# Causal term of the diagonal blocks on VectorE, and closing products right behind the input products

## The reference

```python
def causal_attention(q, k, v):          # 12 heads, q and k 96 wide (64 + 32 rotated), v 64 wide
    ...
    sc = jnp.einsum('bqhd,bkhd->bhqk', q_blk, k) * scale
    mask = k_pos[None, :] <= q_pos[:, None]
    p = jax.nn.softmax(jnp.where(mask[None, None], sc, -jnp.inf), axis=-1)
    return jnp.einsum('bhqk,bkhd->bqhd', p, v)

def rg_lru_branch(u, ...):              # 768 channels, 6 tiles of 128
    ...                                 # xc: causal convolution with 4 taps
    r = jax.nn.sigmoid(xb @ w_r + b_r)
    i = jax.nn.sigmoid(xb @ w_i + b_i)
    log_a = (-8.0 * softplus(-lam)) * r
    gated_x = jnp.sqrt(-jnp.expm1(2.0 * log_a)) * (i * xc)
    # h_t = exp(log_a)_t * h_{t-1} + gated_x_t
```

## Time and profile before

| | |
|---|---|
| median of 3 runs | 3370.74 us (3360.85 to 3375.93) |
| the profiled execution: its own time, its span | 3378.57 us, 3376.4 us |
| busy share of the span: PE, DVE, ACT, POOL | 91%, 39%, 29%, 24% |
| mean granted clock of PE | 0.941 of full speed |
| token attention, first rotation to last product | 2419 to 2820 us |
| inputs and closing products of the recurrent layer | 2999 to 3169 us |

### The profile page before, as it was taken

One profiled execution on the slowest core, in us unless ns is written; L12 is line 12 of the kernel. 1 busy time (PEld: TensorE's weight loads), 2 busy tenths in 40 slices (PEclk: granted clock), 3 DMA queues, 4 the chain that ended last, 5 costly groups with the idle time before them and its releaser, 6 DMA issues. The chain is left out here.

```text
span 3376.4 us, 33623 instructions
## 1 busy us (share of the span) xinstructions
PE 3083.4 (91%) x14024; PEld 2306.9 (68%) x14024; DVE 1305.8 (39%) x1342; ACT 974.6 (29%) x1262; POOL 808.8 (24%) x380
## 2 busy tenths in 40 slices
PE   8899999999989798899999999898699999888896
PEld 3677777877766476688888787676466666666555
DVE  5153111333426443300000245321656663539455
ACT  3232222212133123311111344231234341336212
POOL 1223111215332122312121345331021111223100
PEclk9999999999989898899999999998799999899898
DMA  9311111252132342111111233312100001120201
GB/s 353 135 51 63 50 50 56 106 174 76 63 138 80 109 167 71 48 50 47 46 45 48 75 125 112 103 56 78 56 20 13 19 20 69 56 75 32 91 13 50
DMA packets 76486, 261.01 MB, mean 77 GB/s; under 512 B 8049, under 2 KB 12385, under 8 KB 75329
## 3 DMA queue, kind: packets, MB, share of 16 engines
q1 hardware_dynamic: 76352, 259.13, 21.8%
HBM read 207.10 MB, written 51.99 MB: 77 GB/s over the span
## 5 line engine op out<-in xcount | busy, mean ns | idle before, releaser
L277 POOL TENSOR_TENSOR w_lo_sb<-raw_w_sb,w_hi_sb 128x1024 fp32r<-128x1024 f32 x231 | 577.9, 2503 | 2061.6 <-ACT w_hi_sb L268 2061.5
L268 ACT ACTIVATE w_hi_sb<-raw_w_sb 128x1024 fp32r<-128x1024 f32 x231 | 243.1, 1052 | 437.7 <-PE ps L285 401.6
L285 PE MATMUL ps<-merged_parts_hi_sb,w_hi_sb 128*128 128x512 f32 x832 | 335.3, 403 | 23.0 <-PEq L500 12.5
L285 PE MATMUL ps<-merged_parts_lo_sb,w_hi_sb 128*128 128x512 f32 x832 | 330.6, 397 | 0.0
L285 PE MATMUL ps<-h_hi_sb,w_hi_sb 128*128 128x512 f32 x720 | 295.7, 411 | 17.7 <-PEq L872 10.7
L285 PE MATMUL ps<-h_lo_sb,w_hi_sb 128*128 128x512 f32 x720 | 288.8, 401 | 0.0
L285 PE MATMUL ps<-merged_parts_hi_sb,w_lo_sb 128*128 128x512 f32 x832 | 275.3, 400 | 0.0
L285 PE MATMUL ps<-h_hi_sb,w_lo_sb 128*128 128x512 f32 x720 | 245.4, 401 | 0.0
L285 PE MATMUL ps<-z_lo,w_hi_sb 128*128 128x512 f32 x512 | 207.3, 405 | 0.0
L285 PEld LDWEIGHTS ps<-merged_parts_hi_sb,w_hi_sb 128*128 128x128 f32 x832 | 158.2, 190 | 67.3 <-issue 19.0
L2732 DVE TENSOR_TENSOR ffn_hidden_sb<-ffn_hidden_sb,ps 128x1024 f32 x20 | 24.4, 1221 | 431.6 <-PE ps L285 431.6
(11 more groups left out here) (571 smaller groups left out, 5579.2 us busy)
## 6 DMA issues: line engine op xcount, KB each, us to landing
raw_w_sb<-in_w SPq DMA_DIRECT2D x231, 512.0 KB, 3.2
ada_w_sb<-in_ada SPq DMA_DIRECT2D x48, 512.0 KB, 6.7
inbox_sb<-gates_out SPq DMA_DIRECT2D x24, 512.0 KB, 4.1
gates_out<-outbox_sb SPq DMA_DIRECT2D x16, 512.0 KB, 2.6
inbox_sb<-sums_out SPq DMA_DIRECT2D x16, 512.0 KB, 4.7
spilled_sum<-x_sb SPq DMA_DIRECT2D x32, 256.0 KB, 2.0
x_sb<-spilled_sum SPq DMA_DIRECT2D x2, 4096.0 KB, 13.7
x_sb<-in_x SPq DMA_DIRECT2D x4, 1024.0 KB, 11.7
```

The lines of the kernel that those rows point to most:

```text
L268: nc.scalar.activation(w_hi[:, n % RING].rearrange("p t m -> p (t m)"), raw_w[:, n % RAW], ACT.Copy).then_inc(w_rounded.sem, 1)
L277: nc.gpsimd.tensor_tensor(w_lo[:, n % RING].rearrange("p t m -> p (t m)"), raw_w[:, n % RAW], flat_hi, ALU.subtract).then_inc(w_split.sem, 1)
L285: mm = nc.tensor.matmul(o, wt, xs, start=start and part == 0 and xs is x_hi, stop=stop and part == 1)
```

## The change

In the attention:
- The mask product of a diagonal step is gone. DVE adds the constant in PSUM instead (`causal_term`), and ACT's Exp of such a step waits for DVE (`causal_s`).
- The steps of the second half take blocks 4 to 7 first, so that the first eight steps of a head are the diagonal ones.
- `weigh` runs two steps behind the scores instead of one, and `maxima` comes ahead of `weigh`.
- The rotation of the queries (`turn_queries`) writes the rounded tile by a sum of its own instead of a cast. For heads 0 and 1 it stays in its place; for the others it moves from P(u+1) into S(u), behind the causal terms of the first two steps.
- DVE's order in S(u): eight causal terms with the rotation behind the second and six maxima behind the last six, `normalise(u, 0)`, the last two maxima.

In the recurrent layer: `closing` is planned from the end of `inputs`, and the roundings and subtractions of `gating` are planned behind the end of the recurrence (`R_END`), in a program of their own on DVE.

```diff
-                steps = [(u, t, s) for u in range(U) for t in range(2) for s in range(4 * t + 4)]
-                last = lambda t: 4 * t + 3
+                blocks = ((0, 1, 2, 3), (4, 5, 6, 7, 0, 1, 2, 3))
+                steps = [(u, t, s) for u in range(U) for t in range(2) for s in blocks[t]]
+                begins = lambda t: 4 * t
+                last = lambda t: 3
...
+                            behind = 2 if causal else 1
...
-                                        diag = causal and s >= 4 * t
-                                        mm = nc.tensor.matmul(ps[:, 4 + n % 2, 0:hi - lo],
-                                                              k_of(u)[0:dq + 1, s * P:(s + 1) * P],
-                                                              q_of(u)[0:dq + 1, lo:hi], start=True, stop=not diag)
-                                        if diag:
-                                            mm = nc.tensor.matmul(ps[:, 4 + n % 2, 0:P], ident, C("mask_kq"),
-                                                                  start=False, stop=True)
-                                        mm.then_inc(pe_s.sem, 1)
+                                        nc.tensor.matmul(ps[:, 4 + n % 2, 0:hi - lo],
+                                                         k_of(u)[0:dq + 1, s * P:(s + 1) * P],
+                                                         q_of(u)[0:dq + 1, lo:hi], start=True, stop=True
+                                                         ).then_inc(pe_s.sem, 1)
                                         if causal and u + 1 < U and n - mine[0] == 1:
                                             turn_values(u + 1)
-                                        if n > mine[0]:
-                                            weigh(n - 1)
                                         if causal and u + 1 < U:
                                             if 2 <= n - mine[0] < 2 + CH:
                                                 maxima(u + 1, n - mine[0] - 2)
+                                        if n - mine[0] >= behind:
+                                            weigh(n - behind)
+                                    if causal:
+                                        weigh(mine[-2])
...
-                                        act.wait_ge(pe_s.sem, val(i, len(steps), b_s + n + 1))
+                                        if on_diagonal[n]:
+                                            act.wait_ge(*causal_s.at(diagonals[n]))
+                                        else:
+                                            act.wait_ge(pe_s.sem, val(i, len(steps), b_s + n + 1))
...
+                            def turn_queries(u):
+                                j = at[("Q", u, 0)]
+                                dve.wait_ge(pe_done.sem, base + j + 1)
+                                q_ = q_of(u)[64:96]
+                                nc.vector.tensor_tensor(q_, pair[j % 2][64:96], rot[64:96], ALU.mult)
+                                link(nc.vector.tensor_tensor(t_b[64:96], pair[j % 2][96:128], rot[96:128], ALU.mult))
+                                link(nc.vector.tensor_tensor(rounded(u)[0][64:96], q_, t_b[64:96], ALU.add))
+                                nc.vector.tensor_tensor(q_, q_, t_b[64:96], ALU.add).then_inc(dve_free.sem, 1)
+                                dve.wait_ge(dve_free.sem, b_e["dve"] + after["dve"][j])
+
+                            def causal_term(n):
+                                dve.wait_ge(pe_s.sem, b_s + n + 1)
+                                nc.vector.tensor_tensor(ps[:, 4 + n % 2, 0:P], ps[:, 4 + n % 2, 0:P], C("mask_kq"), ALU.add
+                                                        ).then_inc(causal_s.sem, 1)
...
-                                    for b in between:
-                                        take_maxima(i, u + 1, b)
+                                    if causal:
+                                        for j in range(CH):
+                                            causal_term(step_at[(u, 0, 0)] + j)
+                                            if 1 < u + 1 < U and j == 1:
+                                                turn_queries(u + 1)
+                                            if u + 1 < U and j >= 2:
+                                                take_maxima(i, u + 1, j - 2)
                                     normalise(i, u, 0)
...
-            C0 = inputs.end + 15.0
+            C0 = inputs.end
+
+            R_END = conv_at[5] + 2.0 + 17.0
...
-                        yield at[m] + 5.0
+                def rest(dve):
+                    for m in range(6):
+                        yield max(at[m] + 5.0, R_END + 1.5 + 0.3 * m)
                         dve.wait_ge(*hi_s.at(m + 1))
...
-                        yield at[m] + 3.5
+                        yield max(at[m] + 3.5, R_END + 0.3 * m)
```

More of the change, by code:

```diff
@@ L3001, in attention @@
             if causal:
-                steps = [(u, t, s) for u in range(U) for t in range(2) for s in range(4 * t + 4)]
-                last = lambda t: 4 * t + 3
+                blocks = ((0, 1, 2, 3), (4, 5, 6, 7, 0, 1, 2, 3))
+                steps = [(u, t, s) for u in range(U) for t in range(2) for s in blocks[t]]
+                begins = lambda t: 4 * t
+                last = lambda t: 3
             else:
                 steps = [(u, t, s) for u in range(U) for t in range(2) for s in range(keys_n // P)]
+                begins = lambda t: 0
                 last = lambda t: keys_n // P - 1
             step_at = {st: n for n, st in enumerate(steps)}
+            on_diagonal = [causal and s >= 4 * t for _, t, s in steps]
+            diagonals = [sum(on_diagonal[:n + 1]) for n in range(len(steps))]
             span = lambda t, s: (max(HALF * t, P * s) if causal else HALF * t, HALF * (t + 1))
@@ L3108, in weigh @@
                                 pe.wait_ge(act_p.sem, val(i, len(steps), b_p + n + 1))
-                                if s == 0 and (g >= 2 or i is not None):
+                                if s == begins(t) and (g >= 2 or i is not None):
                                     pe.wait_ge(dve_o.sem, val(i, 2 * U, b_do + g - 1))
                                 nc.tensor.matmul(ps[:, 6 + t, lo - HALF * t:HALF], v_of(u, s), pr[:, n % 4, 0:hi - lo],
-                                                 start=(s == 0), stop=(s == last(t))).then_inc(pe_o.sem, 1)
+                                                 start=(s == begins(t)), stop=(s == last(t))).then_inc(pe_o.sem, 1)
                             def turn_values(u):
@@ L3226, in body @@
                                             take_part(i, "V", u + 1)
-                                        if causal and u % 2 == 0 and n == step_at[(u, 1, 4)]:
+                                        if causal and u % 2 == 0 and n == step_at[(u, 1, 0)]:
                                             gating.high(act, u // 2)
@@ L3290, in body @@
                                 if kind == "S":
-                                    between = range(2) if causal and u + 1 < U else ()
-                                    for b in between:
-                                        take_maxima(i, u + 1, b)
+                                    if causal:
[5 more added lines that the diff above has]
+                                                take_maxima(i, u + 1, j - 2)
                                     normalise(i, u, 0)
-                                    if between:
-                                        for b in range(2, CH):
+                                    if causal and u + 1 < U:
+                                        for b in range(CH - 2, CH):
                                             take_maxima(i, u + 1, b)
```

18 lines of the change are left out of this document (6 added, 12 removed).

## The result

Five runs of the changed kernel have a median of 3399.0 us (3392.0 to 3403.07), five of the kernel before on the same chip 3371.9 (3360.85 to 3377.93): ratio 1.0083, interval 1.0066 to 1.0099, so it is slower by 27 to 28 us, 0.8%. The profiled execution took 3392.0 us, its span is 3390.2 us; that of before took 3378.57.

The account below looks back on a forecast made before the run. TensorE, busy for 91% of the span, was taken to bound the kernel. Attention +13.3 us, clock loss +28 and closing products -12.9 summed to +28 on the median of 3370.74: 3399 us, range 3371 to 3414.

Parts of the forecast that it names:

- The moved rotation: Attention: sums wait for GpSimd, so the next head's first row-maximum product comes 8.0 or 10.05 us behind the first score product.
- The idle: Attention: TensorE stands 3.9 or 6.0 us before the next head's first row-maximum product, some 50 us over ten heads.
- Causal terms: Attention: eight VectorE additions a head, 0.3 us each, hidden under TensorE's work; a second wait of 0.85 us goes.
- The clock: Attention: idling drops TensorE's clock for 7 us, costing 2.8 us in each of ten heads, +28 us.
- The stage without the clock: Attention: periods of 32.4 or 34.45 us against 31.75, +16.1 us over heads 1 to 9.
- Heads 0, 10 and 11: Ends of the attention: -2.7 us for head 0, 0 for head 10, -1.2 for head 11.
- Closing tiles: Recurrent layer: closing products fill TensorE's wait, -12.9 us, between 10 and 14.
- no loss of clock: Rival, attention: sums take turns with GpSimd but idling costs no clock; 3371 us, chance 0.12.
- sums that don't wait for POOL: Rival, attention: rotation sums run free of GpSimd, idle 3.0 us; 3351 us, or 3365 with some clock loss; chance 0.12.
- a closing edit that doesn't gain: Rival, recurrent layer: the recurrence is held and TensorE stands at the third closing tile; 3405 to 3412 us, chance 0.06.
- the rival with the loss in the odd heads alone: Rival, attention: the clock drops only in the five odd heads; 3385 us, chance 0.08.
- two spells of half clock: Rival, attention: longer spells of half clock, two per head; 3420 us and more, chance 0.04.

Follow-up runs that it names:

- psum_sums_linked: The changed kernel with the rotation's second product sent to PSUM, so both sums have only one SBUF operand; 3376.62 us, ratio 1.0021.
- filled: The changed kernel plus useless score products (six in odd heads, four in even) in TensorE's wait before the first row-maximum product; 3371.19 us, ratio 1.0006.
- closing_only: The kernel before with the recurrent layer's edit alone, attention untouched; 3357.95 us, ratio 0.9959.
- early_weigh_first: The changed kernel with a PSUM operand in both sums, rotation products before the causal terms, weighing before row-maximum products; 3328.74 us (0.9878), rerun 3331.85.
- early_filled: The changed kernel with a PSUM operand in both sums, rotation products early, one useless 0.86 us product in TensorE's wait; 3357.55 us, ratio 0.9958.
- masks_on_pe: `early_weigh_first` with the causal term back on TensorE as a mask product, orders kept; 3338.74 us (0.9904), rerun 3339.66.

## Why the prediction was right

It gave 3399, and 3399.0 was measured; the change is +27.1 for +28. Point by point, with the predicted value first:

- **The moved rotation.** M0 8.0 (even heads) and 10.05 us (odd) behind S0: 8.0 and 10.0. The rounded sum 2.1 us, the sum in place 1.2 or 3.3: 2.04, and 1.22 or 3.24. `psum_sums_linked` took the cause away and the long sums with it. Here the rule of the Trainium skill ("GPSIMD Engine Reference", Specifications), that the two engines share SBUF interfaces when VectorE has two SBUF inputs, held as far as it goes: with one input in PSUM no instruction was held. That a whole instruction is waited for is not in that section; the rows of this kernel show it.
- **The idle.** 3.9 and 6.0 us: 3.67 and 5.70, 46.8 in ten heads for "some 50".
- **Causal terms** hidden, at 0.3 us each: 0.299 on the mean of 96. No wait ahead of M4. Right, though the prediction put that wait at 0.85 us where the earlier trace rows has 0.69.
- **The clock.** 28 us: by `filled` 24 in the stage of the profiles, 26 by the ratios, 28 by the medians. The 7 us behind M0 ran at 0.59 and 0.66 (the estimate had 0.59 for all), a loss of 2.9 and 2.4 us a head.
- **The stage without the clock.** Periods less that loss are 34.2 and 32.2, for 34.45 and 32.4 predicted. Over heads 1 to 9 that is 5 x 2.4 + 4 x 0.5 = 14 for the predicted 16.1.
- **Heads 0, 10 and 11**, where the two profiles and the working disagree. With the nine periods at 5 x (37.07 - 31.75) + 4 x (34.60 - 31.75) = 38.0, 42.6 - 38.0 = +4.6 us are left for these three heads, where the terms had -2.7, +2.8 and -1.2, together -1.1. The windows above show where it lies: the first 13 us of head 0 ran at 0.54, for 0.86 in the same place before, 4.2 us; and head 11 lost 3.4 behind an idle of 2.03 us, in a place that kept 1.00 before behind 2.62 us. The two make 7.6, for 5.7 that are missing. But this can't be put down to the change: `closing_only`, with the attention of before, had 0.54 and 0.55 in the same two places, and its stage took 371.1 us for 364.0. Against that profile the three heads are 2.3 us shorter, near the terms. So the profiled execution of before was a mild one there, and the 1.00 of the earlier trace rows is of that execution alone. The same two places lost clock in `filled` (0.53 over its first 13 us, 0.51 over 7 us of head 11): its stage is 382.3 us, 18.3 above before; less 4.3 and 3.4 that is 10.6, where the terms without the clock have 16.1 - 2.7 - 1.2 = 12.2.
- **Closing tiles.** -12.9, between 10 and 14: -12.6 in the profile, -13.9 when alone. The end 74.6 us behind the first gate product of tile 4: 74.2. The recurrence's end, thought to be some 3 us later (2 to 3), is 4.3 later (41.4 us behind that gate product, 37.2 before), and as foreseen nothing waits for it.

The rivals fall one by one: no loss of clock (`filled` shows what that looks like, and the changed kernel isn't it); sums that don't wait for POOL (3.24 us); a closing edit that doesn't gain (`closing_only`). Of the rival with the loss in the odd heads alone nothing is left either, the even ones ran at 0.66. Nor did any of the ten heads have two spells of half clock. That the total fits to the microsecond is partly luck: between the two profiles the three heads at the ends were off by +5.7 and the nine periods by -3.3, and the stages of the two profiles add up to 44.5 - 12.6 = +31.9 where the medians differ by 27.1, which is within what single executions differ by.

## What to carry to other kernels

Taking work off the engine that bounds can be undone by the order that comes with it: 21 us of mask products were gone, and yet a head took 34.3 or 32.3 us at the full clock (`filled`) instead of 31.75, and 26 to 28 us more were lost to the clock, while the same edit with the rotation's products put early, its sums freed of GpSimd and W0 in the wait made a kernel 41 us faster than before, 14 of them by the closing tiles. A chain of VectorE on which TensorE waits should have one operand in PSUM in each instruction that may meet GpSimd. Ahead of any place where TensorE will wait, put dense work of the kernel's own rather than behind it.

## What the runs showed of the hardware that was not expected

- The length of an idle stretch does not decide by itself whether the granted clock falls. At one place of the same attention, ahead of head 11, it stayed at 1.00 behind 2.60 us and was 0.55 behind 2.81 us (`closing_only`). Ahead of M0 it fell in ten of ten heads with a wait of 2.9 us, and in ten of ten with 1.47 us.
- It can fall with no wait at all just ahead of it. In all four heads of `early_weigh_first` that lost it, and in two of the six of `early_filled`, it fell 3.9 to 5.0 us behind S0, before the wait for M0 began, though PE had stood for only 0.19 us since S0 in the head shown. The turning of V, sixteen products of 64x64 in 2.0 us, had just run there. It can't be the whole reason: it runs at that place in the kernel before and in `masks_on_pe` too, and both kept 1.00 in all ten heads. Head 11 of the changed kernel lost the clock behind 2.03 us with no such products directly ahead. None of this was tried by itself. Nor is it clear why a useless product of 0.86 us at that place gave 5 to 8 us and W0, as long, 34, of which only 8.6 are W0's own time, no longer spent behind M0.
- A causal term of 128x128, one operand and the result in PSUM, the other in SBUF, costs DVE 0.299 us (0.298 to 0.300 in 96).
- Two profiled executions differed by 14.5 us in code that is the same in both, about as much as the whole spread of runs of the kernel before.
